# Feed-forward activations turned by block transposes and row-spreading transfers

## What is computed

```python
def swiglu(h, w_gate_up, w_down):
    g, u = jnp.split(h @ w_gate_up, 2, axis=-1)
    return (jax.nn.silu(g) * u) @ w_down
```

## Time and profile before

| | us |
|---|---|
| runs | 1060.05, 1060.62, 1060.73; median 1060.62 |
| span of the profiled execution | 1059.6 |
| PE busy | 1049.6 (99%) |
| DVE busy | 658.3 (62%) |
| ACT busy | 567.9 (54%) |
| POOL busy | 78.7 (7%) |
| weight loads, issue to landing, median | 4.4 |

### The profile page before, as it was taken

One profiled execution on the slowest core, in us unless ns is written; L12 is line 12 of the kernel. 1 busy time (PEld: TensorE's weight loads), 2 busy tenths in 40 slices (PEclk: granted clock), 3 DMA queues, 4 the chain that ended last, 5 costly groups with the idle time before them and its releaser, 6 DMA issues.

```text
span 1059.6 us, 14790 instructions
## 1 busy us (share of the span) xinstructions
PE 1049.6 (99%) x5023; PEld 861.5 (81%) x5023; DVE 658.3 (62%) x953; ACT 567.9 (54%) x920; POOL 78.7 (7%) x170
## 2 busy tenths in 40 slices
PE   9999999999999999999999999999999999999997
PEld 6999888888887788888888888888887688888886
DVE  5867855546687874554567455556777675555543
ACT  5755644445577664444556444454666844444543
POOL 0035100000012040000001000000101200000000
PEclk9999999999999999999999999999999999999999
DMA  8574656555653454646565465646543253656541
GB/s 341 179 238 137 204 171 216 164 198 188 204 182 107 135 181 160 222 159 209 184 200 186 165 210 164 218 160 219 184 154 100 97 181 120 215 162 218 166 152 40
DMA packets 51882, 187.78 MB, mean 177 GB/s; under 512 B 5808, under 2 KB 5952, under 8 KB 51840
## 3 DMA queue, kind: packets, MB, share of 16 engines
q1 hardware_dynamic: 50688, 183.79, 52.1%
q0 software_dynamic: 864, 3.07, 1.0%
q10 hardware_dynamic: 288, 0.37, 0.1%
HBM read 186.15 MB, written 1.05 MB: 177 GB/s over the span
## 4 chain that ended last, share of the span: by engine, by line
PE 95%; DVE 3%; ACT 1%; POOL 0%; DMA 0%; issue 0%; DVEq 0%; SPq 0%
PE pG L1684 17%; PE pG L1686 17%; PE pG L1685 17%; PE pD L1684 12%; PE pD L1686 11%; PE pD L1685 11%; PE pT L1689 3%; PE pG L1689 1%; PE pG L1706 1%; DVE w_low L1341 1%; PE pG L1942 1%; PE pT L1827 1%; PE pD L1689 1%; PE pD L1695 0%; PE pD L1961 0%; PE pG L1988 0%
## 5 line engine op out<-in xcount | busy, mean ns | idle before, releaser
L1341 DVE TENSOR_TENSOR w_low<-raw,w_high 128x1024 fp32r<-128x1024 f32 x340 | 410.9, 1224 | 118.5 <-ACT w_high L1055 105.7
L1055 ACT ACTIVATE w_high<-raw 128x1024 fp32r<-128x1024 f32 x340 | 353.8, 1055 | 81.5 <-PE pG L1686 66.5
L1684 PE MATMUL pG<-w_high,xTh 128*128 128x512 f32 (+1 forms) x816 | 320.1, 392 | 0.1
L1686 PE MATMUL pG<-w_high,xTl 128*128 128x512 f32 (+1 forms) x816 | 312.5, 383 | 0.0
L1685 PE MATMUL pG<-w_low,xTh 128*128 128x512 f32 (+1 forms) x816 | 312.1, 382 | 0.0
L1686 PEld LDWEIGHTS pG<-w_high,xTl 128*128 128x128 f32 x816 | 153.1, 188 | 28.3
L1685 PEld LDWEIGHTS pG<-w_low,xTh 128*128 128x128 f32 x816 | 153.6, 188 | 25.7
L1684 PEld LDWEIGHTS pG<-w_high,xTh 128*128 128x128 f32 x816 | 153.2, 188 | 25.6 <-DVE xTl L1374 0.3
L1684 PE MATMUL pD<-w_high,aTh 128*128 128x512 f32 x384 | 150.8, 393 | 0.0
L1686 PE MATMUL pD<-w_high,aTl 128*128 128x512 f32 x384 | 149.9, 390 | 0.0
L1685 PE MATMUL pD<-w_low,aTh 128*128 128x512 f32 x384 | 149.4, 389 | 0.0
(11 more groups left out here) (272 smaller groups left out, 799.4 us busy)
## 6 DMA issues: line engine op xcount, KB each, us to landing
raw<-in_stream SPq DMA_DIRECT2D x340, 512.0 KB, 4.4
post<-in_posts POOLq DMA_DIRECT2D x5, 512.0 KB, 5.1
early<-in_stream SPq DMA_DIRECT2D x4, 512.0 KB, 12.3
first_w<-in_stream SPq DMA_DIRECT2D x3, 512.0 KB, 5.8
h<-in_x SPq DMA_DIRECT2D x2, 512.0 KB, 5.4
out<-hg SPq DMA_DIRECT2D x3, 256.0 KB, 2.2
consts<-in_consts POOLq DMA_DIRECT2D x1, 417.0 KB, 3.8
out<-hg ACTq DMA_DIRECT2D x1, 256.0 KB, 2.9
```

The costliest lines, as they stand in the source:

```text
L1055: sc.activation(w_high[:, slot(static):slot(static) + CHUNK], raw_of(static), ACT.Copy).then_inc(w_high_done, 1)
L1341: ve.tensor_tensor(w_low[:, slot(static):slot(static) + CHUNK], raw_of(static), w_high[:, slot(static):slot(static) + CHUNK].bitcast(F32), ...
L1684: pe.matmul(dst, ah, hi, start=start, stop=False)
L1686: return pe.matmul(dst, al, hi, start=False, stop=stop)
```

## The change

TensorE doesn't turn the activations of the feed-forwards any more, but for one (row tile 1, last block of FFN4). DVE, behind its multiplication, waits for its own result and transposes each 32x32 block of act into a new buffer aB[t]. SyncE then issues four transfers, each of 32 partitions of aB x 256 floats to 128 partitions x 64 floats of a new buffer aF[t]: a row of 256 floats becomes four rows of 64 (256 bytes). ACT and DVE make aTh and aTl from aF instead of from pT. This puts the hidden features in another order on the partitions, so the rows of the down weights are permuted on the host, and the one turn left on TensorE gets its act with permuted columns.

The order of steps changes with it. T of the feed-forwards is now a step of ACT and DVE alone: T(0,b+1) stands behind G(1,b), and T(1,b) behind G(0,b+2). G(t,b) on TensorE waits for act of block b-1, as T no longer does. SyncE follows the walk: its loads are issued at the fill and R steps of the chunks four before, its transfers of aB at the G steps. The transfers wait for aB_ready.

The core of the diff (the mixer's walk, renamed and without the feed-forward's branches, is left out; `fill`, `start` and `finish` of SyncE issue what they issued before):

```diff
+def walk_ffn_step(ph, s, shift, step, freed, open_end=None):
+    step("G", 0, s, shift)
+    if s == 0:
+        if open_end:
+            open_end()
+            refill(step, freed, 1)
+            step("join", 1, ph.index - 1)
+            step("T", 0, 0, shift)
+            refill(step, freed, 2)
+        else:
+            walk_prep(step, 1, ph.index)
+            step("T", 0, 0, shift)
+            refill(step, freed)
+        return
+    if s == 1 and open_end:
+        walk_prep(step, 1, ph.index)
+    if s >= 2:
+        step("T", 1, s - 2, shift)
+    step("D", 0, s - 1, shift)
+    refill(step, freed)
+    walk_ffn_follower(ph, s - 1, shift, step)
+def walk_ffn_follower(ph, b, shift, step):
+    g, first, last = ph.g_chunk(b), b == 0, b == ph.nb - 1
+    early = 2 if first else 3
+    step("R", g, early, shift)
+    step("G", 1, b, shift)
+    if not last:
+        step("T", 0, b + 1, shift)
+    step("R", g + early, ph.cg - early, shift)
+    if not first:
+        step("D", 1, b - 1, shift)
+    if not first and not last:
+        step("R", ph.d_chunk(b - 1), ph.kd, shift)
+def walk_ffn(eng, ph, step, trips, freed, open_end=None):
     per = RING // (ph.cg + ph.kd)
-    start = 3 if trips else ph.nb
-    for s in range(start):
-        walk_block_step(ph, s, 0, step, freed, open_end)
-    if trips:
-        with eng.Fori(0, trips) as turn:
-            for s in range(start, start + per):
-                walk_block_step(ph, s, turn, step, freed)
-        for s in range(start + per * trips, ph.nb):
-            walk_block_step(ph, s, 0, step, freed)
+    for s in range(3):
+        walk_ffn_step(ph, s, 0, step, freed, open_end)
+    with eng.Fori(0, trips) as turn:
+        for s in range(3, 3 + per):
+            walk_ffn_step(ph, s, turn, step, freed)
+    for s in range(3 + per * trips, ph.nb):
+        walk_ffn_step(ph, s, 0, step, freed)
...
     if ph is FFN4:
-        walk_follower(ph, last, 0, step, freed)
+        step("T", 1, last - 1, 0)
+        walk_ffn_follower(ph, last, 0, step)
+        step("T", 1, last, 0)
         step("D", 0, last, 0)
         step("D", 1, last, 0)
         step("finish",)
         return
     step("D", 0, last, 0)
     step("tail", 0, ph.index)
+    step("T", 1, last - 1, 0)
     step("join", 0, ph.index)
     walk_last_follower(ph, step, freed)
...
+        def moved_by_pe(ph, t, b):
+            return ph is FFN4 and t == 1 and b == ph.nb - 1
+        def turned_act(ph, t, b):
+            if moved_by_pe(ph, t, b):
+                return pT[t][:, 0:256].rearrange("p (k a r) -> p k a r", k=2, a=4)
+            return aF[t][:].rearrange("p (a k r) -> p k a r", a=4, k=2)
+        def ffn_block(ph, b, shift):
+            return ph.first_block - MIX.nb + b + 1 + shift * (RING // (ph.cg + ph.kd))
...
+            def load_behind(c, shift):
+                if c >= RAW and c < RAW + EARLY:
+                    return
+                n = c + (RAW + EARLY if c < RAW else RAW)
+                if n >= N_CHUNKS:
+                    return
+                sp.wait_ge(w_split, c + 1 + shift * RING)
+                src = stream[FIRST + n] if isinstance(shift, int) else stream[bass.ds(shift * RING + (FIRST + n), 1)].rearrange("o p n -> p (o n)")
+                sp.dma_start(raw_of(n), src).then_inc(w_loaded[n % RAW], 16)
+            def fill(first, n, ph):
+                for c in range(first, first + n):
+                    load_behind(c, 0)
+            def refill(first, n, shift, ph):
+                for c in range(first + RING, first + RING + n):
+                    if c < N_CHUNKS:
+                        load_behind(c, shift)
+            def G(t, b, shift, ph):
+                if ph.mixer or moved_by_pe(ph, t, b):
+                    return
+                sp.wait_ge(aB_ready[t], ffn_block(ph, b, shift))
+                for a in range(4):
+                    sp.dma_start(aF[t][:, 64 * a:64 * a + 64], aB[t][32 * a:32 * a + 32, :]).then_inc(aF_moved[t], 16)
...
-                    sc.activation(aTh[t][:].rearrange("p k r -> p (k r)"), pT[t][:, 0:256], ACT.Copy).then_inc(ah_ready[t], 1)
+                    if t == 1 and b:
+                        sc.wait_ge(w_freed, freed_by(ph, b - 1, True) + shift * RING)
+                    if moved_by_pe(ph, t, b):
+                        sc.wait_ge(actT_psum[t], MIX.nb + 1)
+                    else:
+                        sc.wait_ge(aF_moved[t], ffn_block(ph, b, shift) * 64)
...
-                    ve.scalar_tensor_tensor(act[t][:], pG[t][:, 256:512], rr[t], gate[t][:],
-                                            ALU.mult, ALU.mult).then_inc(act_ready[t], 1)
+                    up, by, dst = pG[t][:, 256:512], gate[t][:], act[t][:]
+                    if moved_by_pe(ph, t, b):
+                        up, by = (x.rearrange("p (i k c) -> p i k c", i=4, k=2) for x in (up, by))
+                        dst = dst.rearrange("p (k c i) -> p i k c", k=2, i=4)
+                    ve.scalar_tensor_tensor(dst, up, rr[t], by, ALU.mult, ALU.mult).then_inc(act_ready[t], 1)
+                    if not moved_by_pe(ph, t, b):
+                        ve.wait_ge(act_ready[t], n)
+                        ve.transpose(aB[t][:], act[t][:]).then_inc(aB_ready[t], 1)
...
-                    ve.tensor_tensor(aTl[t][:].rearrange("p k r -> p (k r)"), pT[t][:, 0:256],
-                                     aTh[t][:].rearrange("p k r -> p (k r)").bitcast(F32), ALU.subtract).then_inc(aT_ready[t], 1)
+                    ve.tensor_tensor(aTl[t][:].rearrange("p k (a r) -> p k a r", a=4), turned_act(ph, t, b),
+                                     aTh[t][:].rearrange("p k (a r) -> p k a r", a=4).bitcast(F32), ALU.subtract).then_inc(aT_ready[t], 1)
...
+                if b and not ph.mixer:
+                    pe.wait_ge(act_ready[t], ph.first_block + b + shift * (RING // (ph.cg + ph.kd)))
...
-                n = ph.first_block + b + 1 + shift * (RING // (ph.cg + ph.kd))
-                pe.wait_ge(act_ready[t], n)
+                if not ph.mixer and not moved_by_pe(ph, t, b):
+                    return
+                pe.wait_ge(act_ready[t], ph.first_block + b + 1)
...
-                row = P * (ph.kd * b + k)
-                found[ph.d_chunk(b) + k] = output[row:row + P]
+                q = np.arange(P)
+                rows = P * b + q if ph.mixer else 2 * P * b + 64 * (q % 4) + 32 * k + q // 4
+                found[ph.d_chunk(b) + k] = output[rows]
```

More of the change, by code:

```diff
@@ L153, in refill, with walk_block_step @@
         step("R", freed.pop(0), 1, 0)
[L156 removed]
+def walk_block_step(ph, s, shift, step, freed):
     def fill(name):
[L159 removed]
+        if (name, s) in FILL:
             step("fill", FILL[name, s], 1)
[L162 removed]
+    if s:
         step("G", 0, s, shift)
[L164 removed]
+    if s == 1:
         step("G", 1, 0, shift)
[L166 to L174, removed]
     if s == 2:
@@ L178, in walk_block_step @@
         fill("Y10")
[L179 to L182, removed]
+        step("Y", 1, 0, shift)
     if s >= 1:
@@ L185, in walk_block_step @@
     fill("D")
-    if not (ph.mixer and s == 0):
+    if s:
         step("T", 0, s, shift)
@@ L210, in walk_follower @@
 def walk_follower(ph, b, shift, step, freed):
-    if ph.mixer and b == 1:
+    if b == 1:
         walk_second_follower(ph, shift, step, freed)
         return
-    g, first, last = ph.g_chunk(b), b == 0, b == ph.nb - 1
-    early = (0 if ph.mixer else 2) if first else 1 if ph.mixer else 3
-    step("R", g, early, shift)
+    g = ph.g_chunk(b)
+    step("R", g, 1, shift)
     step("G", 1, b, shift)
[L219 to L231, removed]
+    step("D", 1, b - 1, shift)
+    if b == ph.nb - 2:
+        step("R", g + 1, 1, shift)
+        freed += [*range(g + 2, g + ph.cg), ph.d_chunk(b - 1)]
+    else:
+        step("R", g + 1, ph.cg - 1, shift)
+    step("T", 1, b, shift)
+    if b < ph.nb - 2:
         step("R", ph.d_chunk(b - 1), ph.kd, shift)
-    if ph.mixer and not first:
-        step("Y", 1, b, shift)
+    step("Y", 1, b, shift)
 def walk_last_follower(ph, step, freed):
@@ L571, in walk @@
     step("fill", 3, 3)
-    walk_phase(eng, MIX, lambda *a: step(*a, ph=MIX), 0, freed)
+    walk_mixer(MIX, lambda *a: step(*a, ph=MIX), freed)
     def end_of(ph):
@@ L580, in end_of_attention @@
         step("tail", 1, B_INDEX)
-    walk_phase(eng, FFN1, lambda *a: step(*a, ph=FFN1), 4, freed, lambda: end_of(MIX))
+    walk_ffn(eng, FFN1, lambda *a: step(*a, ph=FFN1), 4, freed, lambda: end_of(MIX))
     walk_attention(lambda *a: step(*a, ph=None), freed, lambda: end_of(FFN1))
-    walk_phase(eng, FFN2, lambda *a: step(*a, ph=FFN2), 4, freed, end_of_attention)
-    walk_phase(eng, FFN3, lambda *a: step(*a, ph=FFN3), 4, freed, lambda: end_of(FFN2))
+    walk_ffn(eng, FFN2, lambda *a: step(*a, ph=FFN2), 4, freed, end_of_attention)
+    walk_ffn(eng, FFN3, lambda *a: step(*a, ph=FFN3), 4, freed, lambda: end_of(FFN2))
```

(11 more changed lines are left out.)

45 lines of the change are left out of this document (30 added, 15 removed).

## The result

The changed kernel takes 1052.22 us (median of four runs, 1051.09 to 1055.01) against 1060.67 (1060.05 to 1061.14) beside it: ratio 0.992, 95% interval 0.991 to 0.994. It is 8.4 us faster; 19.5 us were forecast (1041.1), and 1052.2 lies outside the range of 1036 to 1049.

A forecast was written before the change was run, and what follows sets the result against it. TensorE, busy 99% of the span, was taken as the bound. 1060.62 less 22.4 us of turns, plus stalls of 1.8, 0.4 and 0.7, gave 1041.1 us, range 1036 to 1049.

The forecast's parts named there:

- The saving of a turn: On TensorE, 87 of 88 feed-forward turns removed at 0.252 us each (0.272 in FFN1): 22.4 us saved.
- DVE's transpose: On DVE, 87 added transposes of 128x256 f32, taken at 0.42 us each with 0.1 for the wait: 45 us.
- The whole detour is hidden in the steady state: In the loops, aTl is ready at +9.7 us and D needs it at +16.3: 6.6 us to spare.
- FFN2's DMA share: In FFN2, the transfers' added rows raise the DMA engines' share from 0.55 to about 0.68.
- A: On DVE, a transpose takes about 1.2 us, changes of stage pay 5 us: 1046 to 1052 us; chance 0.10.
- B: Transfers land late, holding ACT and weight splits in the steady state; at 10 us landing, 1097 us; chance 0.06.
- C: DMA engines bind: at 161 ns a row a step takes 19.6 us instead of 16.83, 1182 us; chance 0.03.
- D: On TensorE, the transposes' full length comes back, 47 us: 1016 us with the stalls; chance 0.01.
- E: No effect, since PE waits at G for act just as at T: 1060 us; chance 0.02.
- One place is shorter: FFN4's first block: At FFN4's start, D(0,0) waits for the detour's parts: a stall of 0.7 us, 0 to 1.8 depending on landing.
- The stalls at the changes of stage: Around FFN1, FFN2 and FFN3, PE waits for xTl at six places: 1.8 us plus 0.4 us.
- My line through longer rows: On the DMA engines, extrapolation 18 + 0.035 x bytes from 4 KB and 2 KB rows: 27 ns for a 256-byte row.

The follow-up runs named there:

- e12_moved_twice: Changed kernel with ten edge blocks turned by TensorE, the last split put back ahead of the refills, and every set of four transfers done twice: 1050.94 us.
- e5: Changed kernel with row tile 1's last split at the ends of FFN1 and FFN3 put back ahead of the three refills: 1049.88 us.
- e4: Changed kernel's order of steps and loads, but TensorE turning every feed-forward block as before: 1067.86 us, ratio 1.0065.
- e7: e4 with row tile 1's last split at the ends put back ahead of the three refills: 1061.82 us, ratio 1.0012.
- e1: Changed kernel with row tile 1's last block of FFN1 and FFN3 turned by TensorE again: 1050.75 us, ratio 0.989.
- e9: e5 with row tile 1's last block of all four feed-forwards turned by TensorE: 1043.75 us, ratio 0.984.
- e11: e9 with the split of (0,0) at the starts of FFN1 to FFN3 moved behind the two refills: 1041.62 us, ratio 0.982.
- e2_edges: Changed kernel with TensorE turning row tile 1's last block of all feed-forwards and row tile 0's blocks 0 and 1 of FFN1 to FFN3: 1049.33 us.
- e3_no_transfers: Changed kernel without the row-spreading transfers, parts made from aB itself, so activations are wrongly placed: 1048.73 us, ratio 0.989.

## Why the prediction was wrong

**Right.** The saving of a turn. I took 0.252 us from the spacing of starts; the half step went from 8.41 to 8.16. The Trainium skill's 275 ns for each of the two transposes ("TensorE: Matmul & The Clock Gate", Part 4) is no price in such a row: by it the half step would have come down to 7.9. DVE's transpose has 0.445 us where I took 0.42, and by the starts in the loops 0.37, since the next pass begins before its end. DVE's busy time rose by 25.1 us, under the 30 to 45 that were to show it: beside that overlap, aTl's pass takes 383 ns from aF where it took 425 from pT. The transfers land after 2.5 us (3.3 taken). "The whole detour is hidden in the steady state" held, with room to spare by e12_moved_twice. FFN2's DMA share is 0.65 (0.68 taken). The fall of rivals A, B, C, D and E is in the same rows.

**The step that failed** is "One place is shorter: FFN4's first block". I used the steady state's due time, two half steps behind, for all other blocks and looked for exceptions at the starts only. At the ends of FFN1 and FFN3 the last block's D(1,10) is due after D(1,9) and six matmuls, some 4 us from the start of D(1,9), where a block of the loops has 16.3. The kernel before had the lines for it, act and D(1,10) at the two ends:

```profile
287.81 0.48 DVE L1458 SCALAR_TENSOR_TENSOR act<-pG,stat,gate 128x256 f32<-128x256 f32 x1
...
292.34 0.39 PE L1684 MATMUL pD<-w_high,aTh 128*128 128x512 f32 x1
...
740.29 0.48 DVE L1458 SCALAR_TENSOR_TENSOR act<-pG,stat,gate 128x256 f32<-128x256 f32 x1 [0.85 <-ACT gate L1144]
...
744.55 0.46 PE L1684 MATMUL pD<-w_high,aTh 128*128 128x512 f32 x1
```

By my own terms the parts are ready 0.52 + 1.5 + 3.3 + 0.95 = 6.3 us behind act: 288.29 + 6.3 = 294.6 against 292.34 - 0.25 = 292.1, and 740.77 + 6.3 = 747.0 against 744.3. That would have given stalls of 2.5 and 2.7 us and a forecast of 1046.3. The measured waits are 2.49 and 2.77. That they agree is luck: in the changed kernel the refills set them, and without the refills (e5) 2.50 us of issue and 2.3 of landing give 2.06 and 2.01. From D(1,8) to D(1,10) the two places lost 3.0 and 2.6 us.

**The order of steps.** The prediction has no term for the moved T of `walk_last_follower`, and so puts it at nothing. The move puts two refills in front of the split on both engines, and e4 against e7 prices that one line at some 6 us (4.5 of waits, and half clock behind one of them). In the changed kernel it hides behind the transfers, and the transfers behind it: putting the line back gives 2.3 us (e5), turning the ends by TensorE 1.5 (e1), both together 1052.2 - 1043.75 = 8.5 (e9). These are comparisons over several sets of runs, and for e1 and e5 alone the intervals of the ratios overlap the changed kernel's, so 1.5 and 2.3 are rough; 8.5 is clear of that. By this the 11.1 us that the forecast missed are 8.5 at the ends, 2.1 at the starts by where T(0,0) stands (e9 to e11), and 0.5 left over.

**Mis-sized terms.** An issue of one of the transfers holds SyncE for 0.60 us, not the 0.33 of a weight load: 2.49 instead of 1.5 for four. The stalls at the changes of stage were put at 2.2 us, and PE's waits for xTl are 3.6, with 0.6 for w_low. The one at FFN4's first block, 0.7, didn't come: landing was short enough, and it appears when the transfers are doubled. I had priced DVE's transpose ahead of xTl, but not that ACT stands 2.54 us at the split of (0,0), with xTh behind it.

**Half clock** was in no step. It costs 1.7 us behind the wait at 292.00, and in the kept traces it stands only behind long waits of PE. It differs from one execution to the next: the four runs of e1_ends take 1048.47, 1050.33, 1051.16 and 1053.62 us at a mean granted clock of 0.998, 0.996, 0.997 and 0.995, and those of the changed kernel run from 1051.09 (0.996) to 1055.01 (0.994). Part of the 8.5 us at the ends is this.

## What to carry to other kernels

A detour that is hidden in the loop has a due time of its own at each edge: list, for the first and the last block of every stage, what the bottleneck engine does between the producer and the consumer, and what the helper engines have queued ahead. When one cause of a wait is taken away and the wait stays, look for a second beside it before giving up the theory; here each alone gave some 2 us and both 8.5. Where a wait moves to another engine, place behind it only what is needed later than what it waits for, or do that work first.

## What the runs showed of the hardware

- A transfer within SBUF from 32 partitions of 1024 bytes to 128 rows of 256 bytes holds SyncE for 602 ns (median of 348) and lands after 1.8 to 4.1 us, median 2.5.
- Its rows are cheap. The queue's share went from 52.1% of 1059.6 us (50688 packets, 183.79 MB, page of the kernel before) to 56.9% of 1050.4: (0.569 x 1050.4 - 0.521 x 1059.6) x 16 / 50112 = 15 ns of an engine for a new packet. 348 x 128 = 44544 of these are the rows of 256 bytes, and by them alone it is 16 ns; the windows of FFN2 give (0.65 x 16.32 - 0.55 x 16.83) / 64 = 21. My line through longer rows had 27. The Trainium skill ("DMA: Bandwidth & Descriptors", Specifications) has transfers below 512 bytes as read-modify-write; charged as two 512-byte rows that was 72 ns, and no row here shows such a price.
- Behind some long waits PE runs at 1.2 GHz for about 3 us. In the kept traces of all 14 kernels PE waited 13 times for aTl by 2.0 us or more, and half clock followed eight of these waits: 292.00 in the changed kernel (waited 2.49), 292.11 and 740.37 in e1_ends (2.51, 2.38), 735.31 in e2_edges (2.38), 735.01 in e3_no_transfers (2.78), 293.48 in e4_order_alone (2.13), 738.21 in e5_end_order (2.01), 870.96 in e12_moved_twice (2.03). It did not follow 740.64 of the changed kernel (2.77), 289.93 in e2_edges (2.49), 289.57 in e3_no_transfers (2.50), 750.10 in e4_order_alone (2.38) and 290.54 in e5_end_order (2.06), nor any of the waits of 1.0 to 1.9 us. The length of the wait alone doesn't decide it; what does stays open.
- DVE transposes the 32x32 blocks of 128x256 f32 in 445 ns, about the time of a plain pass over the same elements (483 for act).
